# A fused hybrid decoder block: the attention stage's side work in another order, first row maxima earlier, retention scores in head pairs, mix transposes moved back

## What is computed

```python
att = jnp.einsum('bhncd,bhnmd->bhncm', qc, kc) * decay[None, :, None]
y_intra = jnp.einsum('bhncm,bhnme->bhnce', att, vc)
...
y = y * lax.rsqrt(jnp.mean(y * y, axis=-1, keepdims=True) + EPS)
...
o = g[0] * o_cmp + g[1] * o_sel + g[2] * o_win
...
mix = jnp.concatenate([y_ret, y_nsa], axis=-1) @ w_out[l]
x = x + ga1 * mix
h2 = rmsnorm(x, ln_ffn_g[l]) * (1.0 + sc2) + sh2
ffn = (jax.nn.silu(h2 @ w_ff_gate[l]) * (h2 @ w_ff_up[l])) @ w_ff_down[l]
```

## Time and profile before

| what | us |
|---|---|
| median of three runs (lowest to highest) | 748.0 (741.95 to 753.46) |
| the profiled execution's own time | 751.32 |
| its span, first to last instruction | 749.5 |
| PE busy in the span | 698.6 (93%) |
| DVE, ACT, POOL busy | 338.1, 224.8, 267.3 |
| mean granted TensorE clock | 0.964 of 2.4 GHz |

### The profile page before, as it was taken

One profiled execution on the slowest core, in us unless ns is written; L12 is line 12 of the kernel. 1 busy time (PEld: TensorE's weight loads), 2 busy tenths in 40 slices (PEclk: granted clock), 3 DMA queues, 4 the chain that ended last, 5 costly groups with the idle time before them and its releaser, 6 DMA issues.

```text
span 749.5 us, 9012 instructions
## 1 busy us (share of the span) xinstructions
PE 698.6 (93%) x3547; PEld 581.3 (78%) x3547; DVE 338.1 (45%) x595; ACT 224.8 (30%) x378; POOL 267.3 (36%) x127
## 2 busy tenths in 40 slices
PE   2788899999989788899999999999999999999995
PEld 1666678987777667888899888888888888888884
DVE  4878999975477673324440110000000018733215
ACT  4435323322232233114353232212222222323222
POOL 2326433431000211207406444443434336464521
PEclk9979999999999899589999999999999999999998
DMA  9965976664000000063403332323332223322002
GB/s 312 358 233 167 349 266 219 210 252 186 29 2 1 1 1 1 0 211 106 134 1 113 94 103 85 112 85 108 88 107 90 92 75 115 112 85 84 1 1 112
DMA packets 73962, 88.09 MB, mean 118 GB/s; under 512 B 3048, under 2 KB 57536, under 8 KB 73792
## 3 DMA queue, kind: packets, MB, share of 16 engines
q1 hardware_dynamic: 73184, 86.36, 35.1%
q0 software_dynamic: 416, 1.08, 0.4%
q10 hardware_dynamic: 320, 0.07, 0.0%
HBM read 85.41 MB, written 2.10 MB: 117 GB/s over the span
## 4 chain that ended last, share of the span: by engine, by line
PE 81%; DVE 9%; ACT 3%; DMA 3%; issue 2%; SPq 1%; POOL 0%; POOLq 0%; DVEq 0%
PE ps L1127 11%; PE ps L1480 11%; PE ps L1482 11%; PE ps L1481 11%; PE ps L1129 11%; PE ps L1128 11%; PE ps L1252 4%; DMA raw<-in_w_in 3%; DVE acc L726 2%; PE ps L1306 2%; PE ps L1296 2%; PE ps L1360 1%; DVE ps L869 1%; PE ps L1140 1%; PE ps L1207 1%
## 5 line engine op out<-in xcount | busy, mean ns | idle before, releaser
L400 POOL TENSOR_TENSOR wl<-raw,wh 128x1024 fp32r<-128x1024 f32 (+1 forms) x94 | 238.3, 2541 | 277.6 <-ACT wh L452 277.5
L452 ACT ACTIVATE wh<-raw 128x1024 fp32r<-128x1024 f32 (+1 forms) x94 | 97.3, 1038 | 157.2 <-PE ps L1482 74.3
L1480 PE MATMUL ps<-hTh,wh 128*128 128x512 f32 (+1 forms) x384 | 142.9, 372 | 0.0
L1481 PE MATMUL ps<-hTl,wh 128*128 128x512 f32 (+1 forms) x384 | 142.8, 372 | 0.0
L1482 PE MATMUL ps<-hTh,wl 128*128 128x512 f32 (+1 forms) x384 | 142.8, 372 | 0.0
L1092 DVE TENSOR_TENSOR act<-ps,sg 128x512 f32<-128x512 f32 x22 | 15.2, 692 | 212.3 <-PE ps L1482 212.3
L1127 PE MATMUL ps<-wh,hTh 128*128 128x512 f32 (+1 forms) x224 | 91.4, 408 | 9.8 <-DVE hTl L764 8.6
L1128 PE MATMUL ps<-wl,hTh 128*128 128x512 f32 (+1 forms) x224 | 87.0, 388 | 0.0
L1129 PE MATMUL ps<-wh,hTl 128*128 128x512 f32 (+1 forms) x224 | 86.9, 388 | 0.0
L1482 PEld LDWEIGHTS ps<-hTh,wl 128*128 128x128 f32 x384 | 72.4, 188 | 12.5
L1481 PEld LDWEIGHTS ps<-hTl,wh 128*128 128x128 f32 x384 | 72.4, 189 | 12.5
(11 more groups left out here) (194 smaller groups left out, 876.8 us busy)
## 6 DMA issues: line engine op xcount, KB each, us to landing
raw<-in_w_ada SPq DMA_DIRECT2D x32, 512.0 KB, 6.3
raw<-in_w_ff_gate SPq DMA_DIRECT2D x22, 512.0 KB, 3.8
raw<-in_w_ff_up SPq DMA_DIRECT2D x22, 512.0 KB, 3.7
raw<-in_w_ff_down SPq DMA_DIRECT2D x22, 512.0 KB, 3.2
raw<-in_w_in SPq DMA_DIRECT2D x20, 512.0 KB, 7.6
early<-in_w_ada SPq DMA_DIRECT2D x16, 512.0 KB, 9.5
raw<-in_w_out SPq DMA_DIRECT2D x8, 512.0 KB, 6.4
xs<-in_x SPq DMA_DIRECT2D x4, 512.0 KB, 5.6
```

The lines of the kernel that those rows point to most:

```text
L400: pool.tensor_tensor(lo, raw[:, slot, 0:n], hi.bitcast(F32), ALU.subtract).then_inc(w_lo, 1)
L452: a.activation(split(u, n)[0], raw[:, slot, 0:n], ACT.Copy).then_inc(w_hi, 1)
L1480: mm(o, hi[:, ks], hTh[:, k, c0:c1], start=k == 0, stop=False)
L1481: mm(o, hi[:, ks], hTl[:, k, c0:c1], start=False, stop=False)
```

## The change

The tables of slots are new, and so is what stands in a slot:

- The maxima of group 1 follow unit 20, those of groups 2 and 3 stand behind and in the middle of units 21 to 23 of the projection (16 pairs, of which 8 were in slots 0 to 5). The two first `max_transpose` stand in the middle of units 20 and 21.
- `ret_scores(i, p)`, `ret_decay(i, p)` and `ret_values(i, p)` take a pair of heads. The scores go to banks 4 and 5, which the pairs of the maxima use too, and no longer to bank 6. The two heads lie on partitions 0 to 63 and 64 to 127. Those of tile 0 are made after unit 22 of the projection, and their decayed result lies in `PT`, so `exp(1)` waits for its values. There are 8 such calls of each kind for 16.
- A new `maxima_free` stands ahead of nearly every user of banks 4 and 5: it waits until DVE has done all that was issued there.
- `mix_transposes` has the slots 7, 18 and 28 for 8, 21 and 34, three or four slots behind its `ret_norm` (slots 4, 14 and 24, for 7, 20 and 33). It also waits for the compressed branch of the next tile, whose banks it takes.
- `cmp_values(i)` waits for `ret_norm` of tile `i-1`. The split of the first four weight units of the output projection comes in slots 16, 20, 26 and 30 for 20, 24, 33 and 37. The load of `decay` is two units earlier in SP's queue.

```diff
+PAIR_AT = {4: [(4, 0)], 5: [(4, 1)], 6: [(4, 2)], 7: [(4, 3)],
...
+MAX_AT = {1: 2, 3: 3, 9: 4, 15: 5, 22: 6, 30: 7}
+CS_AT = {9: 2, 20: 3}
+CT_AT = {11: 2, 22: 3}
+CO_AT = {0: 1, 15: 2, 25: 3}
+RS_AT = {8: (1, 0), 10: (1, 1), 18: (2, 0), 20: (2, 1), 26: (3, 0), 28: (3, 1)}
+RV_AT = {1: [(0, 0), (0, 1)], 10: [(1, 0)], 11: [(1, 1)], 20: [(2, 0)], 21: [(2, 1)], 30: [(3, 0)], 31: [(3, 1)]}
+SQ_AT = {2: 0, 12: 1, 22: 2, 32: 3}
+NORM_AT = {4: 0, 14: 1, 24: 2, 34: 3}
+M_AT = {7: 0, 18: 1, 28: 2}
+OUT_AT = {16: 0, 20: 1, 26: 2, 30: 3}
...
-                if (kind, j) == ("w", U0_OUT + 2):
+                if (kind, j) == ("w", U0_OUT):
...
+                    if n == 1:
+                        a.wait_ge(r_y, 2)
...
+            def ret_decay(i, p):
+                d.wait_ge(r_s, 2 if i == 0 else 2 * i + p + 1)
...
+                if i > 1:
+                    d.wait_ge(r_y, 2 * (i - 1) + p + 1)
...
+                d.tensor_tensor(ats(i, p)[:, :, 0:i + 1], ps[:, 4:6, c0:c0 + w].rearrange("p a (j q) -> p a j q", q=P),
...
+            def maxima_free():
+
+                for kind, s_ in (("pair", mx_min), ("block", mb_ok), ("decay", r_dec)):
+                    if issued[kind]:
+                        pe.wait_ge(s_, issued[kind])
...
+                else:
+                    pe.wait_ge(r_norm, i)
...
+                for j in range(i + 1):
+                    for a_ in range(2):
+                        r_ = slice(a_ * RDK, (a_ + 1) * RDK)
+                        ins = mm(ps[:, 4 + a_, c0 + j * P:c0 + (j + 1) * P], rkT[r_, p, j * P:(j + 1) * P],
+                                 rqT[r_, p, i * P:(i + 1) * P], start=True, stop=True)
...
+                if i < TT - 1:
+                    pe.wait_ge(c_mix, i + 2)
+                    pe.wait_ge(cT_ok, i + 2)
```

More of the change, by code:

```diff
@@ L218, in block_kernel, with ats @@
         ident = cst[:, K_ID:K_ID + P]
-        def ats(h, j):
-            return hTf[:, 4 * (h % 2) + j, (TT - 1) * P:T]
+        def ats(i, p):
+            if i == 0:
+                return PT[:, 1, p, 0:2 * P].rearrange("p (a j q) -> p a j q", a=2, j=1)
+            return hTf[:, p, :, (TT - 1) * P:T].rearrange("p (a j) q -> p a j q", a=2)
         rope = cst[:, K_ROPE:K_ROPE + TT * P].rearrange("p (t n) -> p t n", t=TT)
@@ L619, in _ @@
                     cmp_copy(CT_AT[n])
-                if n - RH - 1 in R_AT:
-                    ret_squares(R_AT.index(n - RH - 1))
+                if n in SQ_AT:
+                    ret_squares(SQ_AT[n])
                 if n in M_AT:
@@ L998, in _ @@
                     mod_rows(9, ga2, 0)
-                if v == 22:
                     for h in range(HPG):
                         row_min(1, h)
+                if v == 22:
+                    max_rows(1)
                     cmp_gates(0)
                     mod_rows(10, ga2, 1)
+                    row_min(2, 0)
+                    row_min(2, 1)
                 if v == 23:
-                    max_rows(1)
+                    row_min(2, 2)
+                    row_min(2, 3)
                     cmp_out(0)
                     cmp_scores(1)
+                    ret_decay(0, 0)
+                    ret_decay(0, 1)
                 for j in ada_after.get(v + 3, []):
                     ada(j)
+            for h in range(HPG):
+                row_min(3, h)
             cmp_gates(1)
@@ L1024, in _ @@
                     cmp_out(CO_AT[n])
[L1025 to L1031, removed]
+                if n in RS_AT:
+                    ret_decay(*RS_AT[n])
+                if n in SQ_AT:
+                    ret_var(SQ_AT[n])
+                if n in NORM_AT:
+                    ret_norm(NORM_AT[n])
                 if n in M_AT:
@@ L1193, in rot_transposes @@
                 ins.then_inc(rotT, 1)
+            issued = {"pair": 0, "block": 0, "decay": 0}
+            def maxima_free():
+                for kind, s_ in (("pair", mx_min), ("block", mb_ok), ("decay", r_dec)):
+                    if issued[kind]:
+                        pe.wait_ge(s_, issued[kind])
             def pair(x, h):
@@ L1200, in pair @@
                 c0 = h * w % T if i < 2 else 0
[L1201 to L1204, removed]
+                if h % (2 if i == 1 else HPG if i == 0 else 1) == 0:
+                    maxima_free()
+                issued["pair"] += 1
                 for g in range(NG):
@@ L1210, in max_transpose @@
             def max_transpose(x):
-                pe.wait_ge(mx_min, pair_count(x, HPG - 1))
+                maxima_free()
+                issued["block"] += 1
                 pe.transpose(ps[:, 4, 0:P], mcol[:, x % 2, :], ident).then_inc(mx_T, 1)
@@ L1324, in _ @@
                         modulation(q + 1)
+                    if v == 20 and t == 3:
+                        max_transpose(0)
+                    if v == 21 and t == 2:
+                        max_transpose(1)
+                    if v == 22 and t == 2:
+                        pair(2, 2)
+                        pair(2, 3)
+                    if v == 23 and t == 2:
+                        pair(3, 0)
+                        pair(3, 1)
                     if ch and q == 0:
@@ L1382, in _ @@
                 if v == 20:
-                    max_transpose(0)
+                    for h in range(HPG):
+                        pair(1, h)
                     cmp_scores(0)
@@ L1386, in _ @@
                 if v == 21:
-                    for h in range(HPG):
-                        pair(1, h)
+                    pair(2, 0)
+                    pair(2, 1)
                     cmp_transposes(0)
@@ L1392, in _ @@
                 if v == 22:
-                    max_transpose(1)
+                    ret_scores(0, 0)
+                    ret_scores(0, 1)
                     cmp_values(0)
@@ L1396, in _ @@
                 if v == 23:
+                    pair(3, 2)
+                    pair(3, 3)
                     cmp_transposes(1)
@@ L1413, in _ @@
                     cmp_values(CO_AT[n])
-                for i, n0 in enumerate(R_AT):
-                    if n0 <= n < n0 + RH:
-                        ret_scores(i, n - n0)
-                    if n0 < n <= n0 + RH:
-                        ret_values(i, n - n0 - 1)
+                if n in RS_AT:
+                    ret_scores(*RS_AT[n])
+                for i, p in RV_AT.get(n, []):
+                    ret_values(i, p)
                 if n in M_AT:
```

57 lines of the change are left out of this document (21 added, 36 removed), and 7 rows, old and new, of the table PAIR_AT.

## The result

| what | before | after |
|---|---|---|
| median of four runs (lowest to highest), us | 748.72 (741.95 to 753.46) | 729.87 (727.62 to 730.25) |
| ratio, 95% interval | | 0.974 [0.970, 0.977] |
| profiled execution, us | 751.32 | 729.54 |
| its span, us | 749.5 | 727.7 |
| mean granted TensorE clock | 0.964 | 0.976 |

A forecast was written before the change was run, and what follows sets the result against it. PE sets the end, losing time in attention to waits for DVE and to half clock. Work 2.45, waits 5.3 and half clock 12.6 us sum to 20.35, taking 751.3 to 731.0 us, range 724 to 744.

The forecast's parts named there:

- work at full clock: Stage and projection ahead of it: 6.3 us of work saved less 3.85 added ahead, 2.45 us gained.
- PE's waits: Attention stage: PE's waits for DVE fall from 14.8 to 9.5 us, 5.3 us gained.
- the new wait in unit 21: Projection: the second max_transpose waits for eight row minima on DVE, 0.65 us.
- two half-clock stretches: Attention stage before: 10 us and 24 us at half clock, costing 12.6 us.
- the norm held beside POOL: Chain into mix_transposes: a DVE operation took 2.32 us for 0.69 while a weight unit's low part ran on POOL.
- I take no saving: Retention head pairs: instructions of 128 columns get no cheaper; bounds 0 and 4.5 us.
- Rival 2: Retention head pairs: the two heads overlap in the array, 4.5 us less, 726.5 us; chance 0.10.
- within 0.1 us of a wait: Attention stage: many of 28 handovers come out this close, so 1.5 us of waits are added to 8.0.
- Half clock 12.6 to 0: Attention stage: the loss to half clock, 12.6 us, goes entirely.
- rival 1: Attention stage, around slots 13 to 15: the clock falls once more, costing 6 to 7 us, 738 us; chance 0.25.
- its two signs: Attention stage: windows show a clock of 1.0 throughout if the forecast holds; a 5 in the clock slices tells against it.
- Rivals 3 and 4: Attention stage: waits only move, 749 us, chance 0.09; DVE becomes the bound through banks 4 and 5, 768.5 us, 0.04.

The follow-up runs named there:

- e4: Kernel before with the second mix_transposes in slot 22 for 21 and the third tile's retention from slot 26 for 27; 740.06 us, ratio 0.987.
- e8: e7 with the retention values of tile 0 in slot 2 for 1; 726.74 us, ratio 0.971.
- e3: Changed kernel with mix_transposes in slots 5, 15 and 25, right behind the norm, for 7, 18 and 28; 737.92 us, ratio 0.983.
- e6: Changed kernel with 16 extra 128-column float32r products in one half of the array, ahead of the first pairs; 731.27 us (one run).
- e1: Changed kernel once more, unaltered, for a second trace; 726.89 us (one run).
- e7: Changed kernel with cmp_values(2) and (3) in slots 17 and 27 for 15 and 25, first squares and norm one slot later; 725.08 us, ratio 0.969.

## Why the prediction was right, and where its terms were not

The time, the sign and the stage's end (311.05 forecast, 309.54 found) came out. The sum has three terms, and they came out like this, in us of the stage:

| term | forecast | measured |
|---|---|---|
| work at full clock | -3.1 | -5.65 |
| PE's waits | -4.65 | -7.0 |
| half clock | -12.6 | -6.2 |
| sum | -20.35 | -18.84 |

The 0.65 us of the new wait in unit 21, which the forecast has under work, counts with the waits here, as the windows do it. The measured column: waits are length less busy. Half clock before is 9.35 (e4) for the second stretch and, with its factor, 6.52 busy us x (1 - 1/1.78) = 2.9 for the first, together 12.2. Half clock after is 6.0 (e8). What is left is work: 145.53 - 12.2 = 133.3 before and 127.65 after. Two errors of 2.5 and 2.3 us to the one side nearly cancel one of 6.4 to the other.

1. *Where the time is lost before: right.* It named two half-clock stretches, priced at 12.6 us and measured at 12.2, and the work at full clock, 104.0 us from 200.0 on, so 133.0 from the first pair, where 133.3 came out. e3 and e4 show that the two waits of `mix_transposes` were the cause of the larger part: taking only those out gains 10.5 us, bringing such waits back loses 8. Distance is what did it. The prediction also named the norm held beside POOL; in the changed kernel all four norms take 0.69 us, but so do e3's, whose waits came back, and e4 kept one held norm and lost the wait. (Of the clock slices it says that all but four have 9 or more; the last slice is an 8 as well, in both pages.)
2. *"I take no saving" for the head pairs: wrong.* This step failed, and by a wrong comparison. It held the 0.058 us of eight instructions by turns against 128 columns at 2.4 GHz, 0.053, and concluded that they ran one after another. What to compare with is the time of a like instruction whose neighbour can't run beside it, and the trace of before had that: float32r products of only 64 columns, on the whole array, start 0.11 us after one another.

```profile
177.19 0.28 PE L1127 MATMUL ps<-KCh,QTh 128*128 128x64 f32 x1
177.30 0.28 PE L1128 MATMUL ps<-KCl,QTh 128*128 128x64 f32 x1
```

Their columns at 2.4 GHz would be 0.027 us, so columns do not give the time of such a short product, and 0.058 was a sign of two at a time. e6 confirms it: 0.115 for one half alone. The retention rows have 0.112 too, but are not quite the same instruction: their operands are float32 and a product shows as two instructions, where the pairs' are float32r and show as one. The rows after: 0.71, 0.94 and 1.06 to 1.16 us for eight, twelve and sixteen, where 1.1, 1.54 and 2.0 were taken: 4.1 us less over seven rows (3 x 0.39 + 2 x 0.60 + 0.94 + 0.84). Rival 2's mechanism is thus what happened, at 4.1 of its 4.5 us, and its test (a row of sixteen: 2.0 or 1.1) told it. The Trainium skill's sentence in "TensorEngine Tiling (Array Packing)", Key Properties, that row tiles load and multiply in parallel, holds here at 128 columns, as e6's rows against the earlier trace rows show; the trace had not spoken against it.
3. *The work moved ahead of the first scores: 0.9 us dearer.* From the first pair to the first scores it was 29.34 us (171.01 to 200.35) and is 33.48 (168.07 to 201.55), 0.40 of it the new wait at the second `max_transpose`, forecast at 0.65. Without it 3.7 more, where 3.2 were forecast, 2.8 with the cheaper retention row. Part of it can be read off the trace: a pair's row in the middle of a unit (188.16 and 197.35) delays the long products around it by 0.63 us, where 0.43 for the row and 0.1 for the restart were counted. The rest was not broken down. Pairs and insertions together should put the work 3.2 us under the forecast, and it is 2.5: 0.7 us is unaccounted for, within what the two bounds of half clock may be off.
4. *The waits: nearly all in the places named.* Slots 1 (0.8 forecast, 0.84 found), 5 (1.0; 0.55), 5 to 7 (1.1; 0.92 in two waits), 14 and 15 (2.25; 1.71), 18 (0.5; 0.58), 21 (0.4; 0.24), 25 (0.85; 0.51), 27 and 28 (1.1; 1.66). Slot 5 was too dear because `max_transpose` arrived just as `ret_var` was done, so DVE's wait for ACT cost PE nothing. The waits named for the slots sum to 7.0 us, for 8.0. Of the 1.5 us for handovers "within 0.1 us of a wait" only one came, 0.40 at 299.37. The test of 9 to 10 us of waits, none over 1.5, thus came out at 7.8 and 1.10.
5. *"Half clock 12.6 to 0": wrong, and this is rival 1.* The clock fell at 219 us and at 243, for 6.0 us. The rival looked for it in slots 13 to 15, and one fall is there; it overlooked slots 5 to 7, where its own sum had 2.1 us of waits and 0.55 + 0.38 + 0.54 came, by the reading of the earlier trace rows that it used for slots 13 to 15. Its price, 6 to 7 us, fits the two falls together. Of its two signs one spoke and one didn't: the granted clock over the stage's attention part is 0.94 and not 1.0 (201.55 to 309.54 us), but the slices show only two eights and no 5, since falls of 7 us are short beside a slice of 18. Singly, e8, e1 and the first execution give 3.4 for the one at 219, which came in all three profiled executions of the changed kernel, and 2.3 to 2.6 for the one at 243, which came in one of them. What decides whether the second comes stays open: the waits ahead of it were the same.
6. *The rest.* `mix_transposes` has no wait in the loop: three slots of distance are enough, and e3 shows what one costs. Nothing from the output projection on changed its length, as the 418.2 us behind the stage say. Rivals 3 and 4 did not happen: the waits fell by half and DVE never held PE for more than 1.10 us.

That 731.0 lies within 1.2 us of the median is therefore partly luck. With the measured terms the sum would be 751.3 - 18.84 = 732.5 us, and the profiled execution after is 2.9 us under that by what lies ahead of the stage.

## What to carry to other kernels

When a long wait and a stretch of half clock stand side by side, the clock can cost more than the wait; move the consumer two or more slots behind its producer, and count on short waits that are left still bringing down the clock now and then. Before saying that two instructions do or don't overlap, compare their rate with that of the same instruction alone, not with a rate worked out from columns and clock. And when a new order puts a product behind an unrelated result only because they share a bank, a slot or two more of distance is worth trying: it gave 2.3 us here for two numbers.

## What was not expected of the hardware

- The two halves of the array overlap at 128 columns: 0.115 us for a float32r product in one half alone, 0.058 with the halves by turns. With all of one half's first and then the other's, rows of 12 and 16 took 1.26 and 1.60 us, between alternation (0.94, 1.06) and one after another (1.54, 2.0). A product can start ahead of one that stands before it in the program: in e6 at 170.35 and 170.51, ahead of 170.56.
- A short float32r product takes longer than its columns at 2.4 GHz: 64 columns on the whole array 0.11 us (for 0.027), 128 columns in one half 0.115 (for 0.053). What the rest of the time is wasn't tested.
- Two executions of one program with waits equal to 0.01 us differ in whether the clock falls at 243 us, worth 2.3 us. In e7 and e8 single runs spread over 8.4 and 7.3 us, and the mean granted clock doesn't explain it: the fastest of each has 0.997, the slowest 0.981 and 0.988, but e7's run of 724.88 us has 0.995 and that of 723.91 has 0.983. One reason is in the traces: the mean also counts a fall between 20 and 40 us, which nine of the twelve profiled executions have (the changed kernel's first with 0.66 there, e1 and e8 with 1.00), and which leaves the first pair where it was (168.07, 167.86 and 168.26 us).
- Half clock made PE's mixed work 1.78 times as long, not twice, over 21 us.
